# PEER coefficient sums laid out in PSUM with the token index innermost

## The reference

```
def one_chunk(xt):                                    # 128 tokens
    ...                                               # s1, s2: scores against two sets of 128 keys
    t1, i1 = lax.top_k(s1, PEER_TOPK)
    t2, i2 = lax.top_k(s2, PEER_TOPK)
    ...
    ts, sel = lax.top_k(cand, PEER_TOPK)
    idx = jnp.take_along_axis(cidx, sel, axis=-1)     # i1 * 128 + i2 of the chosen pairs
    g = jax.nn.softmax(ts, axis=-1)
    act = jax.nn.gelu(jnp.einsum('chkd,cd->chk', u[idx], xt))
    coef = (g * act.astype(jnp.float32)).astype(xt.dtype)
    return jnp.einsum('chk,chkd->cd', coef, v[idx])
```

## Time and profile before

| | us |
|---|---|
| median of three runs | 2233.77 |
| the three runs | 2229.9 to 2234.21 |
| the profiled execution | 2235.31 |
| its span | 2234.0 |
| PE busy (share of the span) | 2157.4 (97%) |
| DVE busy | 1668.3 (75%) |
| ACT busy | 1162.0 (52%) |
| POOL busy | 628.0 (28%) |

### The profile page before, as it was taken

How to read it: one execution, slowest core, us unless ns; L and a number is a source line. 1 busy time by engine, 2 the same in 40 slices (tenths; PEclk the granted TensorE clock), 3 DMA queues, 4 the chain that set the end, 5 groups by cost and what they waited for, 6 DMA issues and landing times.

```text
span 2234.0 us, 44756 instructions
## 1 busy us (share of the span) xinstructions
PE 2157.4 (97%) x18600; PEld 2118.6 (95%) x18600; DVE 1668.3 (75%) x2729; ACT 1162.0 (52%) x1980; POOL 628.0 (28%) x510
## 2 busy tenths in 40 slices
PE   9999999999999999999999999989999999999997
PEld 8898999999999999999999999879999999899997
DVE  6887767898998499975558656997665864787764
ACT  5776565454333433444455455746454544566443
POOL 7422244232222322223335003864002100112001
PEclk8999999999999999999999999999999999999999
DMA  5442445555444544455555554205554555544553
GB/s 168 148 133 95 160 166 170 187 176 173 154 144 155 173 150 148 152 170 189 180 182 170 189 190 138 89 21 161 193 193 151 188 184 192 179 138 148 192 196 114
DMA packets 101144, 357.36 MB, mean 160 GB/s; under 512 B 12048, under 2 KB 15440, under 8 KB 100816
## 3 DMA queue, kind: packets, MB, share of 16 engines
q1 hardware_dynamic: 100080, 352.35, 47.6%
q10 hardware_dynamic: 864, 2.16, 0.3%
HBM read 352.86 MB, written 1.05 MB: 158 GB/s over the span
## 4 chain that ended last, share of the span: by engine, by line
PE 68%; DVE 21%; ACT 3%; POOL 3%; issue 2%; DMA 1%; SPq 0%; POOLq 0%; DVEq 0%; ACTq 0%
PE PS L319 68%; DVE wlo L407 5%; DVE act L1849 3%; POOL dgl L2973 2%; DVE act L1840 2%; DVE ohB L1840 1%; DVE act L1835 1%; DMA raw<-stream 1%; DVE ohA L1835 1%; ACT whi L327 1%; DVE c L330 1%; DVE H L2647 1%; DVE bn L2598 1%; DVE w L2712 1%; DVE H L2645 1%
## 5 line engine op out<-in xcount | busy, mean ns | idle before, releaser
L407 DVE TENSOR_TENSOR wlo<-raw,whi 128x1024 fp32r<-128x1024 f32 x546 | 689.7, 1267 | 205.0 <-ACT whi L327 204.3
L327 ACT ACTIVATE whi<-raw 128x1024 fp32r<-128x1024 f32 (+1 forms) x667 | 698.9, 1050 | 193.9 <-PE PS L319 107.6
L319 PE MATMUL PS<-bn,whi 128*128 128x256 f32 x3328 | 597.0, 281 | 16.6 <-ACT bn L327 4.9
L319 PEld LDWEIGHTS PS<-bn,whi 128*128 128x128 f32 x3328 | 511.1, 188 | 22.5 <-issue 12.2
L319 PE MATMUL PS<-n,whi 128*128 128x256 f32 (+1 forms) x2784 | 520.1, 288 | 8.9 <-DVE wlo L407 3.7
L407 POOL TENSOR_TENSOR wlo<-raw,whi 128x1024 fp32r<-128x1024 f32 x119 | 322.2, 2707 | 718.4 <-ACT whi L327 716.5
L319 PE MATMUL PS<-bn,wlo 128*128 128x256 f32 x1664 | 459.6, 280 | 0.0
L319 PEld LDWEIGHTS PS<-n,whi 128*128 128x128 f32 x2784 | 439.3, 194 | 12.7 <-issue 4.1
L319 PE MATMUL PS<-n,wlo 128*128 128x256 f32 (+1 forms) x1392 | 397.3, 285 | 0.0
L319 PE MATMUL PS<-c,whi 128*128 128x256 f32 x2048 | 372.3, 284 | 0.0
L319 PEld LDWEIGHTS PS<-c,whi 128*128 128x128 f32 x2048 | 318.9, 192 | 0.0
(11 more groups left out here) (351 smaller groups left out, 3037.2 us busy)
## 6 DMA issues: line engine op xcount, KB each, us to landing
raw<-stream SPq DMA_DIRECT2D x666, 512.0 KB, 3.4
abias<-c_alibi ACTq DMA_DIRECT2D x1, 1536.0 KB, 6.3
H<-xt SPq DMA_DIRECT2D x4, 256.0 KB, 7.2
out<-H SPq DMA_DIRECT2D x3, 256.0 KB, 2.4
mask<-c_mask SPq DMA_DIRECT2D x1, 272.0 KB, 7.1
K<-Vh SPq DMA_DIRECT2D x2, 136.0 KB, 4.0
K<-Vl SPq DMA_DIRECT2D x2, 136.0 KB, 5.1
out<-H ACTq DMA_DIRECT2D x2, 128.0 KB, 1.9
```

What stands on the lines that cost most here:

```text
L319: return self.nc.tensor.matmul(out, l, r, start=start, stop=stop, skip_group_check=True)
L327: return self.nc.scalar.activation(out, in_, func, **kw)
L407: k.s[q].inc(me.e.tensor_tensor(lo[:, :], raw[:, :], hi[:, :].bitcast(F32), ALU.subtract))
```

## The change

The sums of a group are written to the bank in the order (i, t): TensorE's output for token x is the 64 words at x, x + 8, x + 16 and so on, where it was the 64 words from 64 x on. The multiplication then walks bank and activations in the order (i, t), so that eight activations stand next to each other, and then the address moves on to the next chunk. Nothing else is changed: the count, the order, the sizes and the waits of all instructions stay as they are on every engine, and no instruction moves.

```diff
@@ coefs in pe_peer
         A, B = p.ohA[half][g % 2], p.ohB[half][g % 2]
+        out = PS[:, 4 + g % 4, :].rearrange("p (i t) -> p t i", t=TG)
         for x in range(TG):
             for q in range(3):
-                ins = k.mm(PS[:, 4 + g % 4, HK * x:HK * x + HK], A[:, x, :], B[q][:, x, :], q == 0 and x == 0, q == 2)
+                ins = k.mm(out[:, x, :], A[:, x, :], B[q][:, x, :], q == 0 and x == 0, q == 2)
         s["cpe"].inc(ins)
@@ multiply in dve_peer
-        v = p.halves[half][:, :].rearrange("p (i t) -> p t i", t=NX)[:, TG * g:TG * g + TG, :]
+        v = p.halves[half][:, :].rearrange("p (i t) -> p i t", t=NX)[:, :, TG * g:TG * g + TG]
         V.wait_ge(s["cpe"], NG * half + g + 1)
         V.wait_ge(s["gelu"], HK * (half + 1))
-        s["coef"].inc(vec.tensor_tensor(v, PS[:, 4 + g % 4, :].rearrange("p (t i) -> p t i", t=TG), v, ALU.mult))
+        s["coef"].inc(vec.tensor_tensor(v, PS[:, 4 + g % 4, :].rearrange("p (i t) -> p i t", t=TG), v, ALU.mult))
```

## The result

| | median, us | runs | span of the profiled execution |
|---|---|---|---|
| before | 2233.99 | 2229.9 to 2236.75 (4) | 2234.0 |
| changed | 2252.84 | 2251.27 to 2254.7 (4) | 2252.6 |

The changed kernel takes 1.0087 times the time of before (95% interval 1.0068 to 1.0105), 18.9 us more. The forecast was 21.7 us more, at 2255.5 us.

What follows compares the result with a forecast made beforehand. PE was taken to bound the kernel, except two coefficient stages bound by DVE. Slower matmul writes (+41.0 us) less PE stalls removed (-19.3 us) gave +21.7 us, a forecast of 2255.5 us, range 2213 to 2264 us.

Steps and rivals of the forecast that it cites:

- The bound: Whole kernel: PE limits, except two coefficient stages where DVE does; ending PE's stalls there wins 19.3 us at most.
- PE's own demand: Two coefficient stages: PE's work without stalls, from timeline spacings, 151.9 us of 161.09 and 185.9 us of 195.96.
- The multiplication: DVE's 64 multiplications: runs of eight as good as dense, 0.60 us for 1.25 us, saving 20.8 us in each stage.
- the step on bursts: DVE's one-hots slowed beside POOL splits: bursts nearly covered, remaining PE stalls costed at 0, at most 5 of 19.3 us.
- The stepped write: PE's 1536 small matmuls writing 8 words apart: factor of 2 on the streaming part, 0.64 us more for each group.
- a factor of 4: Small matmuls' stepped write: far end of the range, read and write of the sums both at half speed.
- The sum: Two coefficient stages: +11.3 and +10.4 us; +41.0 for bursts and -19.3 for stalls make +21.7 us.
- the chances: Whole time: factor of 2 or near it gets 0.60, with its own range 2246 to 2264 us.
- B: Rival: TensorE's stepped write is free, only the -19.3 us stand, 2214.5 us, or 2219 with stalls left; chance 0.20.
- C: Rival: partial write cost that balances, burst grows 0.23 to 0.37 us, time 2229 to 2238 us; chance 0.07.
- D: Rival: stepped write much worse than factor 2; 2337 us at factor 4, 2296 us at factor 3; chance 0.10.
- E: Rival: DVE's multiplication gets no faster, still 1.25 us; 2234 us with a free write, chance 0.03 for that.

Runs made afterwards that it cites:

- e2: Kernel before with only DVE's half of the change: multiplication walks runs of eight activations, matmul writes stay dense; 2214.82 us, 0.9921 times before.
- e4: Kernel before with matmuls writing pairs of words from even words, 16 words on after each, and multiplication over runs of eight; 2213.85 us, 0.9918 times before.
- e5: Kernel before with two tokens interleaved: matmuls write every second word, multiplication walks runs of two activations; 2252.34 us, 1.0086 times before.
- e7: Changed kernel with matmuls writing pairs that start at odd words, straddling two 8-byte lines, wrong sums pairing; 2246.43 us, one run.
- e8: Changed kernel with matmuls writing 64 words densely from an odd word on, wrong sums pairing; 2218.32 us, one run.
- e6: Changed kernel with every small matmul overwriting the bank instead of adding, sums lost; 2253.18 us, one run.
- e1: Kernel before with only TensorE's half of the change: small matmuls write 8 words apart, multiplication as before; 2252.47 us, 1.0090 times before.
- e3: Kernel before with dense matmul writes in order (t, i), multiplication over runs of eight stepping 64 words in PSUM; 2214.27 us, 0.9916 times before.

## Why the prediction was right

**The bound.** The reading that DVE limits the two stages and PE the rest held. e2 leaves the bursts at 0.71 us and shortens the multiplication, and 18.5 us go; the forecast's most was 19.3 us. PE's own demand, added up from spacings of its timeline, was right within 0.4 us in the first stage (151.9 for 151.54) and 1.2 us in the second (185.9 for 187.08).

**The multiplication.** 0.60 us was taken from dense rows and its duration forecast near 680 ns; it is 684. The saving on DVE as a whole was put too high: 20.8 us in each stage, against 10.0 and 16.8 in e2 and 14.0 and 18.8 in the changed kernel. The term took the rest of DVE's work as fixed, while in the first stage of e2 the work beside POOL's splits grew. The forecast also took it that a split meets the three scaled one-hots. In the first stage of the kernel before that is so for 5 of the 14 instructions held up, and the other 9 are one-hots of A (line 1835). The time did not show any of this. In e2 PE waits for 0.8 us in all, which is what the step on bursts said (at most 5 us left), though with 2.6 us of DVE's time to spare in the first stage, not the 13.8 that it had worked out.

**The stepped write.** The term that decided the sign had no row of its own, any more than the runs of eight had. It was taken as a factor of 2 on the part that streams, 0.64 us for a group, and measured as 1.32 - 0.71 = 0.61 us. The choice rested on the nearest row, a multiplication that pays 1.97 for lone words in SBUF. That was an analogy and not a mechanism, and that its size came out within 0.03 us is luck. The reason had to be supplied by the runs: TensorE's write costs by lines of two words (e4, e5, e7, e8), and DVE's walk through SBUF is nearly at full rate with runs of two (e5). e6 takes away the reason that the forecast gave for a factor of 4, an extra price for read and write.

**The sum.** Forecast +11.3 and +10.4 us, measured +9.6 and +8.8. Of the 3.3 us between them, 1.9 are the burst (64 x 0.03 us). The rest is mainly rounding. With 1052 matmuls of 0.12 us, 32 bursts of 1.32 us and 31 times 0.08 us behind a burst the first stage comes to 171.0 us, and with the spacing of 190.00 / 1586 = 0.1198 us to 170.8; it lasted 170.72. One bound in the chances is off as well: a factor of 1.8 with all stalls gone gives 2233.8 + 0.8 x 41.0 - 19.3 = 2247.3 us, not 2246. Nothing hangs on it.

**The rivals.** B was the right price list with the wrong write; e2 gives it to 0.3 us. C and D fell with the burst. E fell with the 684 ns, and e1 shows what was said beside it, that with the slow write the multiplication's speed doesn't matter.

## What to carry to other kernels

A step has to be somewhere when two engines want a tile in different orders, so put it where it is free: here in DVE's read of PSUM (e3), which gives the change's gain without its price, 19 us below the kernel before where the change is 19 us above it. Where a matmul's output must be interleaved, interleave pairs of words that start on an even word (e4 against e7). And before paying anything on the bounding engine to relieve another, work out both engines' demand stage by stage: here the relief could bring 19.3 us at most, so a price of 0.30 us for each group was already too much.

## What the runs showed of the hardware that was not expected

- A matmul's write to PSUM goes by lines of two fp32 words. 24 matmuls of 64 columns take 0.71 us with 32 lines each, 0.73 us with 33, and 1.32 us with 64. Lone words cost the same 2 or 8 words apart, and, 8 apart, whether the matmul adds or overwrites. Only bf16 matmuls of 64 columns at the full clock were measured; the 256-column f32 ones were not tried with a step.
- DVE read PSUM with a step of 64 words (e3) and of 2 (e4) at the dense rate (683 ns for 512 elements). In SBUF it pays for lone words (1329 ns) and hardly for runs of two (708 ns).
- A DVE instruction with one operand in PSUM and one in SBUF runs beside a POOL split at its usual length. One with both in SBUF that starts while a split runs can take up to 2.2 us longer; one that was under way before the split began kept its length. So shortening the former can give less than its own time: 10.0 of 18.5 us in the first stage of e2, but 16.8 of 19.5 in the second.
